# Reordering the projections' rows, the odd layer's blocks and a few edges in a two-layer hybrid encoder step

## The reference

```
even layer:
  h = rmsnorm(x); z = h @ w_in -> aq, ak, av, bq, bk, bv, blr, gate
  ao = banded attention with sinks (16 heads)           # rows 0..7 of y
  bo = rmsnorm(gated linear attention, 4 heads)         # rows 8..15 of y
  x = x + (concat(ao, bo) * silu(gate)) @ w_out         # out-projection, 16 rows
odd layer:
  h = rmsnorm(x); xb, gate = split(h @ w_in)            # 12 blocks of 128 channels each
  u = conv4(xb); r, i = sigmoid(blockdiag(u)) twice
  a = exp(-8 r softplus(-lambda)); b = sqrt(1 - a^2) * i * u
  hs = scan(a, b); x = x + (hs * silu(gate)) @ w_out    # out-projection, 12 rows
y = rmsnorm(x)
```

## Time and profile before

| | us |
|---|---|
| median of 3 runs | 1514.13 |
| lowest, highest | 1512.57, 1516.56 |
| profiled execution | 1512.56 |
| its span | 1510.5 |
| VectorE busy | 831.0 (55%) |
| ScalarE busy | 459.0 (30%) |
| GpSimd busy | 694.8 (46%) |

### The profile page before, as it was taken

How to read it: one execution, slowest core, us unless ns; L and a number is a source line. 1 busy time by engine, 2 the same in 40 slices (tenths; PEclk the granted TensorE clock), 3 DMA queues, 4 the chain that set the end, 5 groups by cost and what they waited for, 6 DMA issues and landing times.

```text
span 1510.5 us, 23502 instructions
## 1 busy us (share of the span) xinstructions
PE 1471.5 (97%) x9312; PEld 1398.5 (93%) x9312; DVE 831.0 (55%) x1206; ACT 459.0 (30%) x780; POOL 694.8 (46%) x457
## 2 busy tenths in 40 slices
PE   7999999999999999999999999989999999989997
PEld 5998888887799999999989999989999999989996
DVE  6114555557655347354394101497888888894114
ACT  5212444445631221221151000325153251560001
POOL 6053222222124334233346444357677685767552
PEclk9999999999999999999999999999999999999998
DMA  5131010101010011100104322111111111122223
GB/s 215 53 96 43 29 46 29 46 29 29 20 38 28 33 49 45 36 28 32 50 28 136 102 80 87 43 56 43 56 56 42 56 56 43 56 73 86 89 83 119
DMA packets 29341, 89.22 MB, mean 59 GB/s; under 512 B 3760, under 2 KB 8784, under 8 KB 29264
## 3 DMA queue, kind: packets, MB, share of 16 engines
q1 hardware_dynamic: 19776, 64.83, 13.2%
q10 hardware_dynamic: 9488, 23.27, 4.8%
HBM read 76.55 MB, written 11.67 MB: 58 GB/s over the span
## 4 chain that ended last, share of the span: by engine, by line
PE 90%; DVE 3%; issue 3%; POOL 3%; ACT 1%; DMA 0%; ACTq 0%; POOLq 0%; DVEq 0%
PE ps L440 53%; PE ps L636 12%; PE ps L486 7%; PE ps L574 2%; PE ps L608 2%; PE ps L595 2%; PE ps L530 2%; PE ps L803 2%; POOL w_hi L398 1%; PE ps L874 1%; POOL w_lo L402 1%; PE ps L711 1%; PE ps L695 1%; PE ps L706 1%; PE ps L685 1%
## 5 line engine op out<-in xcount | busy, mean ns | idle before, releaser
L398 POOL TENSOR_TENSOR w_hi<-raw,ones 128x512 fp32r<-128x512 f32 x216 | 323.2, 1496 | 758.9 <-PE ps L440 415.9
L440 PE MATMUL ps<-H,w_hi 128*128 128x364 f32 (+1 forms) x2532 | 512.9, 330 | 10.0 <-DVE Yr L1721 6.0
L440 PEld LDWEIGHTS ps<-H,w_hi 128*128 128x128 f32 x2532 | 433.2, 189 | 12.6 <-issue 9.4
L402 POOL TENSOR_TENSOR w_lo<-raw,w_hi 128x512 fp32r<-128x512 f32 x216 | 342.9, 1588 | 16.9
L440 PE MATMUL ps<-H,w_lo 128*128 128x364 f32 (+1 forms) x1584 | 349.4, 329 | 0.0
L440 PEld LDWEIGHTS ps<-H,w_lo 128*128 128x128 f32 x1584 | 275.8, 189 | 0.0
L636 PE MATMUL ps<-H,w_hi 128*128 128x364 f32 (+1 forms) x672 | 144.2, 338 | 0.0
L440 PE MATMUL ps<-Yr,w_hi 128*128 128x364 f32 (+1 forms) x636 | 141.4, 331 | 0.0
L486 PE MATMUL ps<-w_hi,H 128*128 128x256 f32 (+1 forms) x720 | 132.3, 284 | 2.9 <-ACT arena L1101 1.7
L1669 DVE TENSOR_TENSOR arena<-ps,arena 128x1092 f32 (+1 forms) x15 | 19.4, 1296 | 199.9 <-PE ps L440 199.9
L636 PEld LDWEIGHTS ps<-H,w_hi 128*128 128x128 f32 x672 | 111.8, 188 | 14.0 <-issue 10.9
(11 more groups left out here) (220 smaller groups left out, 1895.2 us busy)
## 6 DMA issues: line engine op xcount, KB each, us to landing
raw<-weights SPq DMA_DIRECT2D x112, 512.0 KB, 3.4
arena<-xT ACTq DMA_DIRECT2D x14, 546.0 KB, 4.8
x_scratch<-arena ACTq DMA_DIRECT2D x8, 546.0 KB, 5.6
arena<-x_scratch ACTq DMA_DIRECT2D x8, 546.0 KB, 3.6
arena<-k_scratch ACTq DMA_DIRECT2D x8, 304.0 KB, 4.6
yT<-arena SPq DMA_DIRECT2D x2, 768.0 KB, 5.0
yT<-arena SPq DMA_DIRECT2D x2, 576.0 KB, 3.5
arena<-xT SPq DMA_DIRECT2D x2, 546.0 KB, 8.3
```

The costliest lines, as they stand in the source:

```text
L398: pool.tensor_tensor(hi[:, cols].rearrange("p (k n) -> p k n", n=P), raw[:, s, cols].rearrange("p (k n) -> p k n", n=P), every_tile_ones, ...
L402: pool.tensor_tensor(lo[:, cols], raw[:, s, cols], hi[:, cols].bitcast(F32), ALU.subtract).then_inc(w_split, 1)
L440: mm = pe.matmul(sets[st][:, c, 0:n_cols], lw[:, s, w], rx[:, k, c * CW:c * CW + n_cols], start=(first and n == 0 and m == 0), stop=(last ...
```

## The change

Four things are done; no matmul is added or taken away.

- The out-projections take the order of the first pair's tiles from two tables (`ROWS_EVEN`, `ROWS_ODD`). The first rows' high parts (two in the even layer, four in the odd) are written to other memory than H while H is still read, and split before the out-projection; ScalarE copies them to H later, and TensorE's second pair and VectorE's residual wait for these copies (`early_copied`).
- In each odd group the gate-path block of m stands ahead of the block-diagonal piece of m; the loads of these pieces are written out in that order. VectorE reads the first gate-path block between two taps of the third convolution block, and the next ones where it read the former. The gate path is kept in its row of Y, so the y chain now waits for ScalarE's tanh first. In the last group the splits of rows 0 to 8 are laid between the steps.
- ScalarE evicts the third value tile of a head ahead of the first head's decays (and of the next head's bias).
- In the last head the scalings stand before row 12 instead of row 10, and the gate and the root move by two rows and one.

The diff, without most of its context lines and with less indentation:

```diff
@@ -97,6 +97,14 @@
+ROWS_EVEN = (((0, 0), (0, 1), (1, 0), (1, 1), (0, 2), (1, 2), (0, 3), (1, 3),
+   (0, 4), (0, 5), (1, 4), (0, 6), (0, 7), (1, 5), (1, 6), (1, 7)),
+  ((0, 0), (0, 1), (0, 2), (0, 3), (1, 0), (0, 4), (1, 1), (0, 5),
+   (1, 2), (0, 6), (1, 3), (0, 7), (1, 4), (1, 5), (1, 6), (1, 7)))
+ROWS_ODD = (((0, 0), (0, 1), (0, 2), (0, 3), (1, 0), (1, 1), (1, 2), (1, 3), (0, 4), (0, 5), (1, 4), (1, 5)),
+  ((0, 0), (0, 1), (0, 2), (1, 0), (1, 1), (1, 2), (0, 3), (1, 3), (0, 4), (1, 4), (0, 5), (1, 5)))
@@ -122,7 +130,7 @@
 def c_use(m, n):
-return 3 + 3 * m + n
+return 3 + 3 * m + (n + 1) % 3
@@ -177,6 +185,10 @@
+early_hi = sb("early_hi", [P, 2, TOK], F32R, at=arena_at)
+early_xc = sb("early_xc", [P, TOK], F32R, at=arena_at + 4 * 6 * TOK)
+early_of = [Yr[:, 15, :], early_xc[:, :], Yr[:, 12, :], Yr[:, 13, :]]
@@ -240,7 +252,6 @@
 U = Y[:, 12:15, :]
-cgz = Y[:, 15, :]
@@ -303,7 +314,7 @@
-y_hi_done, y_lo_done = sem("y_hi_done"), sem("y_lo_done")
+y_hi_done, y_lo_done, early_copied = sem("y_hi_done"), sem("y_lo_done"), sem("early_copied")
@@ -351,13 +362,18 @@
+  def gate_path_first(n):
+    g, k = divmod(n - PC_C, C_PCS)
+    return n if k < 3 or g > 3 else n + 1 if k % 2 else n - 1
...
   load_run(PC_C - 5, PC_C + 1, by_block(PC_C))
-  load_run(PC_C + 1, PIECES - 5)
+  load_run(PC_C + 1, PC_OO + 1, gate_path_first)
+  load_run(PC_OO + 1, PIECES - 5)
@@ -745,7 +761,7 @@
-  def out_projection(kt, base, use, ready, last_apart):
+  def out_projection(kt, base, use, ready, last_apart, rows, early, copied):
@@ -753,14 +769,11 @@
         if first:
-          for k in range(3):
-            out_tile(0, kt, half, k, piece, ready)
-          for k in range(kt):
-            if k + 3 < kt:
-              out_tile(0, kt, half, k + 3, piece, ready)
-            if k == 0 and not half:
+          for s, k in rows[half]:
+            if (s, k) == (1, 0) and not half:
               pe.wait_ge(drained[1], use[1])
-            out_tile(1, kt, half, k, piece + 1, ready)
+            hi = early[k] if not half and k < len(early) else H[:, half * kt + k, :]
+            out_tile(s, kt, half, k, piece + s, ready, hi)
@@ -768,6 +781,7 @@
     pair(0, True)
+    pe.wait_ge(early_copied, copied)
@@ -777,14 +791,22 @@
-  def out_tile(s, kt, half, k, piece, ready):
+  def out_tile(s, kt, half, k, piece, ready, hi):
     row = half * kt + k
-    mm = project(1 - s, [row], piece, H, Yr, s, first=(row == 0), last=(row == 2 * kt - 1), at0=k,
-          ready=(y_lo_done, ready))
+    if k % 4 == 0:
+      pe.wait_ge(w_split, 2 * piece + (k // 4 - 1))
+    pe.wait_ge(y_lo_done, ready + row + 1)
+    w = slice(k * P, (k + 1) * P)
+    for m, (lw, rx) in enumerate(((w_hi, hi), (w_lo, hi), (w_hi, Yr[:, row, :]))):
+      for c in range(NCH):
+        mm = pe.matmul(sets[s][:, c, 0:cw(c)], lw[:, 1 - s, w], rx[:, c * CW:c * CW + cw(c)],
+               start=(row == 0 and m == 0), stop=(row == 2 * kt - 1 and m == 2))
+    if k == 3:
+      mm.then_inc(half_done, 1)
...
-  out_projection(8, PC_OE, USE_OE, 0, 1)
+  out_projection(8, PC_OE, USE_OE, 0, 1, ROWS_EVEN, [early_hi[:, k, :] for k in range(2)], 2)
@@ -835,15 +857,15 @@
       kts = ((0, 1), (0, 1, 2), (1, 2))[m]
+      v = c_use(m, 2)
+      in_block(p, v % 2, piece + 3 + 2 * m, u[v % 2] + v // 2)
...
           pe.wait_ge(u_lo_done, G + 2 + m)
-        project((p + 2 * m) % 2, kts, piece + 3 + 2 * m, U_hi, U_lo, v % 2, at0=4 * n,
+        project(1 - p, kts, piece + 4 + 2 * m, U_hi, U_lo, v % 2, at0=4 * n,
             half_end=None, wide=True).then_inc(piece_done if n else half_done, 1)
-      v = c_use(m, 2)
-      in_block((p + 1 + 2 * m) % 2, v % 2, piece + 4 + 2 * m, u[v % 2] + v // 2)
@@ -899,7 +921,7 @@
-  out_projection(6, PC_OO, USE_OO, MIX, 1)
+  out_projection(6, PC_OO, USE_OO, MIX, 1, ROWS_ODD, early_of, 6)
@@ -1101,8 +1123,8 @@
-  values(0, 0)
-  values(0, 1)
+  for t in range(3):
+    values(0, t)
@@ -1111,7 +1133,7 @@
       act.wait_ge(bias_ready, i + 2)
-    for t in range(2, NT):
+    for t in range(3, NT):
@@ -1147,15 +1169,18 @@
       act.wait_ge(b_done, i + 1)
-      values(i + 1, 0)
-      values(i + 1, 1)
+      for t in range(3):
+        values(i + 1, t)
...
+    act.wait_ge(q_ready, B_HEADS)
+    for k in range(2):
+      act.activation(early_hi[:, k, :], Y[:, k, :], ACT.Copy).then_inc(y_hi_done, 1)
     act.wait_ge(piece_done, PC_OE)
-    for k in range(MIX):
-      if k == 2:
+    for k in range(2, MIX):
+      if k == 4:
         gate_tanh_b(1)
-      if k == 4:
+      if k == 5:
@@ -1164,6 +1189,8 @@
   head(B_HEADS - 1, True)
+  for k in range(2):
+    act.activation(H[:, k, :], early_hi[:, k, :].bitcast(F32), ACT.Copy).then_inc(early_copied, 1)
@@ -1209,6 +1236,9 @@
+  def early_high(k):
+    act.activation(early_of[k], Y[:, k, :], ACT.Copy).then_inc(y_hi_done, 1)
@@ -1226,10 +1256,14 @@
       vr, vi, vg = (c_use(m, n) for n in range(3))
-      act.wait_ge(half_done, piece + 4 + 2 * m)
+      if last and m == 2:
+        act.wait_ge(piece_done, piece + 8)
+        mix_high(4)
+        mix_high(5)
+      act.wait_ge(half_done, piece + 5 + 2 * m)
...
        .then_inc(drained[vr % 2], 1)
-      act.wait_ge(piece_done, piece + 4 + 2 * m)
+      act.wait_ge(piece_done, piece + 5 + 2 * m)
@@ -1239,26 +1273,40 @@
       act.activation(aa, tr, ACT.Exp, bias=cur_n[:, m, 0:1], scale=cur_n[:, m, 0:1]).then_inc(c_a, 1)
+      if last and m == 2:
+        mix_high(6)
...
       act.activation(sa, aa, ACT.Square).then_inc(c_a, 1)
+      if last and m == 2:
+        mix_high(7)
...
       act.activation(th, th, ACT.Sqrt).then_inc(c_sqrt, 1)
+      if last and m == 0:
+        act.wait_ge(cvo_done, G + 3)
+        early_high(0)
+        early_high(1)
+      if last and m == 1:
+        act.wait_ge(c_iu, G + 2)
+        early_high(3)
       if last and m == 2:
-        act.wait_ge(piece_done, PC_OO)
-        mix_high(0)
-        mix_high(1)
+        mix_high(8)
...
       act.wait_ge(drained[vg % 2], u[vg % 2] + vg // 2 + 1)
-      act.activation(gc, cgz, ACT.Tanh, scale=0.5).then_inc(c_tanh, 1)
+      act.activation(gc, slot(Y, G + m), ACT.Tanh, scale=0.5).then_inc(c_tanh, 1)
+      if last and m == 0:
+        act.wait_ge(c_iu, G + 1)
+        early_high(2)
...
   group(KC // 3 - 1, True)
-  with act.Fori(2, KC - 1) as k:
+  with act.Fori(9, KC - 1) as k:
     mix_high(k)
+  for k in range(4):
+    act.activation(H[:, k, :], early_of[k].bitcast(F32), ACT.Copy).then_inc(early_copied, 1)
@@ -1532,7 +1580,8 @@
     dve.wait_ge(y_hi_done, k + 1)
-    dve.tensor_tensor(Yr[:, k, :], Y[:, k, :], H[:, k, :].bitcast(F32), ALU.subtract)\
+    hi = early_hi if k < 2 else H
+    dve.tensor_tensor(Yr[:, k, :], Y[:, k, :], hi[:, k, :].bitcast(F32), ALU.subtract)\
@@ -1618,6 +1667,9 @@
     gate(0)
+    if last:
+      split_mix(0)
+      split_mix(1)
@@ -1643,13 +1695,14 @@
-    for k in range(MIX):
+    for k in range(2, MIX):
...
         mean_square()
+      if k == 4:
...
         root_inverse()
-      if k == 10:
+      if k == 12:
@@ -1674,6 +1727,7 @@
+    dve.wait_ge(early_copied, 2 if n == 1 else 6)
@@ -1716,6 +1770,11 @@
   dve.wait_ge(rb_done, 2)
+  def early_rest(k):
+    dve.wait_ge(y_hi_done, MIX + k + 1)
+    dve.tensor_tensor(Yr[:, k, :], Y[:, k, :], early_of[k].bitcast(F32), ALU.subtract)\
+     .then_inc(y_lo_done, 1)
@@ -1729,6 +1788,13 @@
+    def gate_in(m):
+      vg = c_use(m, 2)
+      dve.wait_ge(piece_done, piece + 4 + 2 * m)
+      dve.tensor_tensor(chunks(slot(Y, G + m)), setv(vg % 2), chunks(rb), ALU.mult)\
+       .then_inc(drained[vg % 2], 1)
@@ -1748,6 +1814,8 @@
                     ALU.mult, ALU.add).then_inc(cv_step if j < 3 else cv_done, 1)
+        if (n, j) == (2, 1):
+          gate_in(0)
@@ -1758,10 +1826,16 @@
+      dve.wait_ge(drained[vi % 2], u[vi % 2] + vi // 2 + 1)
+      dve.scalar_tensor_tensor(ti, ti, 1.0, U[:, m, :], ALU.add, ALU.mult).then_inc(c_iu, 1)
+      if last and m == 2:
+        mix_rest(4)
...
       dve.scalar_tensor_tensor(th, sa, 1.0, th, ALU.add, ALU.mult).then_inc(c_w, 1)
-      dve.wait_ge(drained[vi % 2], u[vi % 2] + vi // 2 + 1)
-      dve.scalar_tensor_tensor(ti, ti, 1.0, U[:, m, :], ALU.add, ALU.mult).then_inc(c_iu, 1)
+      if last and m == 1:
+        early_rest(1)
+      if last and m == 2:
+        mix_rest(5)
@@ -1769,32 +1843,39 @@
       dve.memset(aa[:, s0 - 1:s0], 0.0).then_inc(c_seam, 1)
-      dve.wait_ge(piece_done, piece + 5 + 2 * m)
-      dve.tensor_tensor(chunks(cgz), setv(vg % 2), chunks(rb), ALU.mult).then_inc(drained[vg % 2], 1)
+      if m < 2:
+        gate_in(m + 1)
+      elif last:
+        mix_rest(6)
...
                  ALU.mult, ALU.add).then_inc(c_scan, 1)
+      if last and m == 1:
+        early_rest(2)
+        early_rest(3)
       if last and m == 2:
-        mix_rest(0)
-        mix_rest(1)
+        mix_rest(7)
+        mix_rest(8)
...
       dve.wait_ge(drained[vg % 2], u[vg % 2] + vg // 2 + 1)
+      dve.wait_ge(c_tanh, G + m + 1)
       y = slot(Y, G + m, 0, SEQ)
```

(9 more changed lines are left out.)

## The result

| | before | after |
|---|---|---|
| median, 5 runs each on one chip, us | 1512.57 (1512.23 to 1516.56) | 1503.45 (1501.06 to 1503.84) |
| profiled execution, its span, us | 1512.56, 1510.5 | 1502.43, 1500.6 |

A forecast was written before the change was run, and what follows sets the result against it. TensorE, busy 97% of the span, was taken as the bound, so only its idle time and clock could move. Gains of 1.8 + 1.1 + 7.0 + 2.6 = 12.5 us gave a forecast of 1501 us, range 1491 to 1508.

The forecast's parts named there:

- A: Value tiles of head 1: evicting the third tile before the decays removes a TensorE wait, gain 1.8 us.
- B: Even out-projection: gross gain 5.7 us, less a new row 12 wait of 3.1 and half clock of 1.5, net 1.1.
- C: Odd groups, gate-path blocks first: the wait before the first group's next block goes, gain 7.0 us, half clock included.
- The rival that an instruction came late: First odd group: the 5.1 us "issue" wait is not VectorE's and stays, about 1508; chance 0.04.
- The chain at a group's end: Odd groups: VectorE's work through the PSUM read takes 22.1 us, TensorE wants the bank at 23.9; no stall, cost 0.
- D: Odd out-projection: gross gain 8.6 us, less 6.0 of stalls for late lower rows, net 2.6.
- The five pieces: Odd out-projection: TensorE stalls for rows 4, 5, 7, 8 and 9, 6.0 us in all.
- The sum: Whole kernel: gains of the four parts, 1.8 + 1.1 + 7.0 + 2.6 = 12.5 us.
- The rival of everything hidden: All four parts: VectorE's turns with GpSimd fall well, no row is late, gain 23.1 us, 1491; chance 0.20.

The follow-up runs named there:

- part A alone: The kernel before with only the third value tile's eviction moved ahead of the decays: 1512.79, ratio 0.9999 (0.9984 to 1.0014).
- mending it: The changed kernel with ScalarE's wait for q one value tile later in the first three heads, so tile 5 is evicted first: 1499.84, ratio 0.9910.
- the kernel with the fixes of A and B: The changed kernel with tile 5 evicted ahead of ScalarE's wait for q and the even out-projection's row 12 asked for later: 1494.25, ratio 0.9874.
- GpSimd's operations made small: The changed kernel with GpSimd splitting only 8 of each 512 weight columns around the starts of both out-projections: 1489.82, ratio 0.9845.

## Why the prediction was right, and where it was not

**A was wrong in sign.** The step that failed: "VectorE's chain to q behind it ends 0.7 later too; TensorE wants it only after the remaining value tiles, so that is free." The start of the decays was forecast rightly. The chain did end 0.7 later, but ScalarE wants q as well, and the evictions of tiles 5 and later stand behind that wait in its queue. Nor is the 0.7 the greater half. In before that eviction ended at 423.36, or 421.15 counted as in after (2.21 for the start); TensorE, no longer held at tile 4, asks at 419.8. Without any lateness some 1.4 of wait would have come; 0.7 makes it 2.1 (the trace: 2.2 from start to start, less the usual 0.12). The old stall had covered this one. The exchange cost 1.8 in the trace with the half clock and 0.2 in the one without (part A alone), against 1.8 forecast as gain; undoing it and mending it both confirmed the sign.

**B was right in each term.** Gross 5.7 forecast, 5.5 with the wait taken away; new wait 3.1 forecast, 3.0 found from start to start, for the row and the reason named; half clock 1.5 forecast, 1.6 found. All six traces with this wait show the half clock.

**C was right:** 7.0. The rival that an instruction came late is out: the 5.1 of "issue" is gone in all kernels with the new order. The chain at a group's end was forecast at 22.1 of 23.9 us, and took 21.7 (end of the small block at 1240.0, PSUM read at 1261.75), with no wait:

```profile
1239.37 0.66 PE L456 MATMUL ps<-ur,w_hi 128*128 128x364 f32 x3
...
1261.53 0.22 DVE L1808 TENSOR_TENSOR arena<-ps,arena 128x64 f32<-128x64 f32 x1
```

But the prediction counted C as 7.0 whatever D did. It is worth that only with D's early rows. C was never taken out alone; its 7.0 is read from the traces.

**D was right in its waits and missed two small terms.** The five pieces were forecast as 0.8, 0.9, 2.4, 0.8, 1.1, 6.0 in all; without half clock (the kernel with the fixes of A and B) they are 1.1, 0.7, 2.3, 0.7, 1.0 from start to start, 5.9 in all. Gross 8.6: found too (8.1 with GpSimd's operations made small, and 0.5 for the hand-over below). Missing were, first, some 0.1 for the slower first matmuls behind each of the waits (0.74 to 0.77 for three instead of 0.66), some 0.4 in all; second, the hand-over to the second pair. In the new order the first PSUM set gets its last tile, row 11 of block 0, one tile before the end and not four, so VectorE's read of it (1.3 us) is late: the gap at 1375.31, 0.5 with its restart, in every kernel with this order. 8.6 - 5.9 - 0.4 - 0.5 = 1.8, and 1.6 was found. A step that reorders tiles has to be followed to who reads the bank, not only to who fills it.

**The sum** of 12.5 would be 7.8 by the changed places. The 2.2 from the start of the profiled execution brought the traces back to 10.0, the medians differ by 9.1. So the time was near in part by luck: the four places gave 4.7 less than forecast, 3.6 of it in A and 1.0 in D, and part of that was made up outside them. The rival of everything hidden (1491) did not come, but two reorderings and seven operations moved off GpSimd reach it (1490.65).

## What to carry to other kernels

When a stall goes, look at the same engine's next demands as if all arrived earlier by the stall, and at everything queued behind the wait that supplies them, on every engine that waits for the delayed result. Where two engines hold each other up, putting one engine's late result first uncovered the other's (rows 7 and 8); asking for the late row later (row 12) and moving operations to a third engine did help. A gain at one place can be worth nothing without the edit at another, so take parts out one at a time.

## What the runs showed of the hardware that was not expected

- A wait of 1.93 us was followed by 3.41 us at 1.2 GHz in one execution (421.89 in after), one of 1.94 in the same place by full clock (part A alone). Of the seven traces with this wait five show the half clock. One profile does not settle whether a wait costs its clock too.
- The same start of the kernel ran with a stretch of half clock at 45.02 or without; the two kinds of start moved all that follows by 2.2 us, a fifth of the gain under study.
- The cost of meeting GpSimd, for an operation of VectorE with two inputs in SBUF, is about 1.1 us each and not in proportion: 0.22 became 1.31. A scan became 3.53 from 2.42, and the GpSimd operation beside it 3.27 where others take 2.2.
